# Recurrence layer: keys and queries in one tensor, and one product of 512 columns per level in place of two of 256

## The reference, cut to what matters

```python
q, f, i, g = jnp.split(h @ w_in, 4, axis=-1)
q = silu(q); f = lb + (1 - lb) * sigmoid(f); logf = log(f); kin = 1 - f
...
def step(state, inp):                       # per chunk, 8 heads, 128 x 128 state
    q_, k_, v_, g_ = inp
    G = jnp.cumsum(g_, axis=2)
    o_inter = einsum('bhtk,bhkv->bhtv', q_ * exp(G), state)
    decay = exp(where(causal, G[t] - G[s], -inf))
    A = einsum('bhtk,bhsk,bhtsk->bhts', q_, k_, decay)
    o = o_inter + einsum('bhts,bhsv->bhtv', A, v_)
    new_state = exp(G_last) * state + einsum('bhsk,bhsv->bhkv', k_ * exp(G_last - G), v_)
```

## Time and profile before

| what | us |
|---|---|
| median of 3 runs | 4051.85 |
| lowest, highest | 4051.05, 4053.05 |
| the profiled execution, its time | 4051.03 |
| the profiled execution, its span from first to last instruction | 4049.2 |
| head stage of the recurrence (2025 to 2220 of the span) | 195 |
| VectorE busy in it | 144.71 |
| TensorE busy in it | 126.16 |
| GpSimd busy in it | 80.14 |
| ScalarE busy in it | 68.18 |

### The profile page before, as it was taken

One profiled execution on the slowest core, in us unless ns is written; L12 is line 12 of the kernel. 1 busy time (PEld: TensorE's weight loads), 2 busy tenths in 40 slices (PEclk: granted clock), 3 DMA queues, 4 the chain that ended last, 5 costly groups with the idle time before them and its releaser, 6 DMA issues. The chain is left out here.

```text
span 4049.2 us, 47658 instructions
## 1 busy us (share of the span) xinstructions
PE 3655.1 (90%) x18444; PEld 2985.0 (74%) x18444; DVE 1669.8 (41%) x2700; ACT 893.6 (22%) x2344; POOL 1906.0 (47%) x749
## 2 busy tenths in 40 slices
PE   8999987487889899999966999998999998889999
PEld 6777864366777688877855888876788877668887
DVE  2323237876546431133376311238321235642113
ACT  2333341112223311111133100116110012421111
POOL 5444431311443256655543566551466553336654
PEclk9999986787999799999978999999999999889999
DMA  3337851133231122222200322231222222122222
GB/s 130 105 100 95 113 80 51 59 78 85 78 106 63 68 93 95 94 94 89 94 10 1 109 94 93 94 104 43 99 94 93 97 92 82 65 79 94 94 98 79
DMA packets 95953, 342.50 MB, mean 85 GB/s; under 512 B 26951, under 2 KB 45639, under 8 KB 61209
## 3 DMA queue, kind: packets, MB, share of 16 engines
q1 hardware_dynamic: 83408, 314.22, 26.0%
q10 hardware_dynamic: 12360, 25.70, 1.8%
HBM read 318.91 MB, written 16.78 MB: 83 GB/s over the span
## 5 line engine op out<-in xcount | busy, mean ns | idle before, releaser
L294 POOL CAST wh<-raw 128x2048 fp32r<-128x2048 f32 x269 | 513.1, 1907 | 1720.0 <-PE bank L336 1355.3
L296 POOL TENSOR_TENSOR wl<-raw,wh 128x2048 fp32r<-128x2048 f32 x269 | 1245.5, 4630 | 21.5
L334 PE MATMUL bank<-XTh,wh 128*128 128x512 f32 (+1 forms) x2448 | 951.9, 389 | 43.7 <-DVE XTl L1167 15.1
L335 PE MATMUL bank<-XTh,wl 128*128 128x512 f32 (+1 forms) x2448 | 936.7, 383 | 0.0
L336 PE MATMUL bank<-XTl,wh 128*128 128x512 f32 (+1 forms) x2448 | 935.8, 382 | 0.0
L334 PEld LDWEIGHTS bank<-XTh,wh 128*128 128x128 f32 x2448 | 468.1, 191 | 155.2 <-issue 42.4
L336 PEld LDWEIGHTS bank<-XTl,wh 128*128 128x128 f32 x2448 | 467.0, 191 | 89.9
L335 PEld LDWEIGHTS bank<-XTh,wl 128*128 128x128 f32 x2448 | 468.3, 191 | 84.2
L334 PE MATMUL bank<-wh,XTh 128*128 128x512 f32 (+2 forms) x1056 | 393.7, 373 | 37.9 <-DVE XTl L1167 12.6
L335 PE MATMUL bank<-wh,HTl 128*128 128x512 f32 x1024 | 403.5, 394 | 0.0
L334 PE MATMUL bank<-wh,HTh 128*128 128x512 f32 x1024 | 401.8, 392 | 0.0
(11 more groups left out here) (341 smaller groups left out, 4138.8 us busy)
## 6 DMA issues: line engine op xcount, KB each, us to landing
raw<-in_weights SPq DMA_DIRECT2D x270, 1024.0 KB, 4.8
B<-bias_d ACTq DMA_DIRECT2D x8, 1024.0 KB, 5.6
B<-bias_a ACTq DMA_DIRECT2D x8, 512.0 KB, 10.8
bias_d<-O SPq DMA_DIRECT2D x16, 256.0 KB, 21.1
MO<-HS SPq DMA_DIRECT2D x64, 64.0 KB, 2.5
bc<-in_ln_g ACTq DMA_DIRECT2D x8, 512.0 KB, 6.6
bc<-in_ln_b ACTq DMA_DIRECT2D x8, 512.0 KB, 7.7
X<-in_x SPq DMA_DIRECT2D x4, 512.0 KB, 8.3
```

The lines of the kernel that those rows point to most:

```text
L294: pool.tensor_copy(wh[s][:, :], raw[r][:, :]).then_inc(w_high.h, 1)
L296: pool.tensor_tensor(wl[s][:, :], raw[r][:, :], wh[s][:, :].bitcast(F32), ALU.subtract).then_inc(w_split.h, 1)
L334: nc.tensor.matmul(psum, sh, mh, start=first, stop=False)
L335: nc.tensor.matmul(psum, sl, mh, start=False, stop=False)
```

## The change

`QF` and `KIN` are no longer two tensors of 8 x 512 columns but the two halves of one tensor `KQ`; both names stay as views of it, so all other code reads the same columns as before. The two half products of a level become one operation of 512 columns. Its first input and output is the whole slot; its second is an access pattern written by hand, which takes for each block half a block from the keys and then half a block from the queries, which lie 8 x 512 columns further on. The link between the two half products is gone; the signal to TensorE (`DW`) hangs on the one operation.

```diff
-                    QF = sb("QF", [P, KT, S], F32, c2)
-                    KIN = sb("KIN", [P, KT, S], F32, c2)
+                    KQ = sb("KQ", [P, 2, KT, S], F32, c2)
+                    KIN, QF = KQ[:, 0], KQ[:, 1]
...
                                     elif n >= 2:
-                                        x3, half = blocks(x, n - 2), P >> (n - 1)
-                                        kin, q = blocks(of(KIN, i, b), n - 2), blocks(of(QF, i, b), n - 2)
-                                        link(v.tensor_tensor(x3[:, :, 0:half], x3[:, :, 0:half], kin[:, :, 0:half], ALU.mult))
-                                        v.tensor_tensor(x3[:, :, half:], x3[:, :, half:], q[:, :, half:], ALU.mult).then_inc(DW.h, 1)
+                                        half, k = P >> (n - 1), KIN[:, 2 * i + b, :]
+                                        x4 = x.rearrange("p (n y c) -> p n y c", y=2, c=half)
+                                        kq = bass.AP(k.tensor, k.offset, [list(k.ap[0]), [2 * half, S // (2 * half)], [KT * S + half, 2], [1, half]])
+                                        v.tensor_tensor(x4, x4, kq, ALU.mult).then_inc(DW.h, 1)
```

## The result

The changed kernel takes 4023.46 us (median of 6 runs, 4017.3 to 4024.74) beside 4051.51 for the kernel before (6 runs, 4048.62 to 4055.81): a ratio of 0.9931, 95% interval 0.992 to 0.9942, or 28 us less. Forecast were 4036 and a range of 4029 to 4045. A second comparison, told at the end of the experiments, gave a smaller ratio: 0.9951, or 20 us less (15 to 26). The head stage itself, from its first merge to its end, was shorter by 25.6 us in one profile and 25.8 in the other.

A forecast was written before the change was run, and what follows sets the result against it. VectorE was taken to set the pace from a head's first merge to the state copies, TensorE afterwards. Five heads 11, the last 1.3, the one before 1.2, the first 2.4: 15.9 us, so 4036; range 4029 to 4045.

The forecast's parts named there:

- the walk: One head followed level by level after the change: product with the queries ends at 13.6 instead of 15.68, gain 2.1.
- T: Start of a head's first merge, from which the prediction counted times within that head; 2105.98 in the head worked out.
- Then TensorE decides: Level 5 of a head: TensorE's group takes 1.82 at its slow clock, so the merge starts at about 6.5.
- (c): Rival: TensorE not slowed in mid-head, its clock at a head's start adding or taking some us; 20 to 24 us, chance 0.17.
- Five heads like it: Heads taken to go like the one worked out: 5 x 2.1 = 10.5, raised to 11 for two losing more to GpSimd.
- what follows is untouched and hangs on that end: After the product with the queries: last merge, low_head, state steps, TensorE's output, transposes and first level keep their length.
- the wait of 4.5 for TensorE unchanged: Sign: VectorE's idle stretch before a head's first merge stays at 4.5 us.
- The first head: Head under nine GpSimd subtractions in a row, second halves caught in three levels: gain taken as 2.4 us.
- The last: Last head, with only two GpSimd subtractions: levels 3 to 7 at 0.20 each plus part of a caught half, 1.3 us.
- (b): Rival: time caught behind GpSimd stays or TensorE takes over the gain; 8 us or down to 6, 4044 to 4046, chance 0.2.
- (d): Rival: the input alternating between two regions is slow at every level; at half rate 21 us lost, 4057; chance 0.08.
- The graded form: Alternating input costs 0.40/512 us per change of region: 0.1 at level 6, 0.2 at level 7; 3 us, 4039.

The follow-up runs named there:

- A second comparison: The changed kernel unaltered, run and profiled a second time against the kernel before: 4023.98 us, ratio 0.9951.
- TensorE busy in mid-head: Kernel before plus matmuls of the identity, result never read, 4 after level 2 and 3 after level 3: ratio 0.9994.
- the halves: The kernel before, with two half products of 256 columns per level and a link between them: 4051.51 us.
- 12 matmuls: Changed kernel plus 12 unread matmuls of the identity after level 8, in TensorE's wait for the state: ratio 0.9915 to the kernel before.
- the whole form: The changed kernel, with one product of 512 columns per level, against the kernel before: 4023.46 us, ratio 0.9931.
- 16 matmuls: Changed kernel plus 16 unread matmuls of the identity after level 8: 4010.17 us, ratio 0.9901 to the kernel before.

## Why the prediction fell short

**Right, and shown.** The single product at levels 3 to 6 followed the walk nearly to the tenth. After T, predicted: merges at 1.38 and 2.90, products ending at 4.50 and 6.02. Measured in the head above: 1.38, 3.01, 4.53 (2099.94 + 0.76) and 5.99. The rule behind it, that whichever of VectorE and GpSimd reads first finishes, fits the runs in which GpSimd only writes, where no product is caught. Also right: the layout costs and gives nothing, level 2 and level 8 add little, GpSimd's delay reaches nobody (VectorE waits for an exponential of the levels only once, for 0.4 us, as in the kernel before), and EL waits for ScalarE by 0.7.

**The step that failed** is "Then TensorE decides: its level-5 group took 1.82 ... Starting at 4.55 it ends at 6.37". I carried TensorE's clock over from one head of the trace of before, though the change alters how long TensorE idles before that group (1.64, 1.20 and 0.40 ahead of levels 3, 4 and 5; after the change 0.78, 0.46 and 0.29). It took 1.16, the merge came at 5.91, not 6.5, EL at 11.45, not 12.0, and the head part was 13.07, not 13.6. That is the case named (c) with 0.17. Five heads like it measured 2.45 to 3.02 each, 13.7 together, where 11 stood in the sum. That keeping TensorE busy makes the group fast is shown by the run with TensorE busy in mid-head, for the halves; for the changed kernel itself it is inferred. The idle time alone doesn't decide it: in the kernel before, the group was slow in the fifth head and fast in the sixth, with nearly the same idle time ahead. Two of the five heads I took as like the one I walked, the second and the sixth, had the fast group already.

The same mistake stands in "what follows is untouched and hangs on that end", and it was the larger: the wait parts and the stretch after the last head hold TensorE's output, transposes and first level, at the clock of the moment, and shrank by 5.0 in one profile and 7.0 in the other. One of the signs I had named, "the wait of 4.5 for TensorE unchanged", came out at 3.70 in the head above.

The 11.6 us between the 15.9 forecast and the 27.5 of the spans are made up of 5.0 in these stretches, 2.7 in the five heads, 2.1 in the other three heads and 1.9 outside the stage, each rounded.

**Mis-sized terms.** The first head gave 3.87, not 2.4: there the pairs at levels 3, 4 and 8 had been caught, at level 3 in both halves, a merge had waited 0.71 for TensorE, and, with no head before it to be copied, its EL doesn't wait for ScalarE, so that level 8 counts too. The last gave 1.80, not 1.3, the one before it 1.31 as against 1.2. The clock at a head's start was named in (c) without a price; it should have had a term of up to 1 in each of seven heads. One operation for two saved 0.165 a level, not 0.20. The level-8 product cost 0.83, not 1.09; beside GpSimd up to 0.96. In the seven heads in which EL waits for ScalarE it is covered.

**Rivals.** (b), that the caught time would stay, is refuted: 14 of 20.65 us are contention that went away (12 of 18.9 by the second profile). (d), slow at every level, is refuted by 0.69 at levels 2 to 7 without GpSimd. The graded form of it also fell: runs of two columns (level 7) take 0.68.

**Left open.** 1.9 us of the profiles' difference lie outside the stage; the whole time scatters by more than that with the same stage, so I ascribe them to nothing. Why 12 matmuls were enough in the halves and not in the whole form wasn't settled; only the number 16 was found to do. What makes TensorE's clock fall in one head and not in the next, after nearly the same idle time, is open too, and so is why the output and the first group ran faster in the changed kernel after the same 4.26 of idle time.

## What to carry to other kernels

- Two short operations in place of one cost their fixed part twice (6.6 us here), and here about twice that sum again in contention (14 us): each start is a chance for another engine's reads to get in first. Price an operation by what can come between it and its neighbour, and try the merged form on all of a loop: in the head parts the levels changed by groups gave 9.7 us, all together 20.65.
- A duration on TensorE is not a constant of the instruction. When a change alters how long TensorE idles ahead of a group, work the sum out at both clocks.
- If an engine must wait a few microseconds each round and its clock falls for it, work without use in the wait can be worth a good part of such a change: 16 matmuls took 10 to 12 us from the wait parts of the changed kernel, beside the 25.6 us that the change took from the stage, and 19 such matmuls per head 18.5 us from the stage of the kernel before.

## What was not expected of the hardware

- An input that alternates column by column between two regions 16 KB apart cost 0.14 more per 512 columns (0.83 against 0.69 beside an idle GpSimd); the stride of 64 elements in the earlier trace rows had cost 0.40. Alternating every two columns cost nothing (0.68).
- Taking away a link between two operations of VectorE saved 0.12 between their starts and nothing in the end.
